# Windowed attention of a two-block fp32 model: stacked query halves, doubled keys, values with both halves side by side

## The reference, cut to what matters

```
q, k, v = jnp.split(h @ w_qkv, [Hq * d, Hq * d + Hkv * d], axis=-1)   # Hq 16, Hkv 4, d 64
q = apply_rope(q...); k = apply_rope(k...)
s = jnp.einsum('bnqhgd,bnchd->bnhgqc', q, kb) * (d ** -0.5)           # kb: 3 blocks of 128 keys
s = jnp.where(|kpos - qpos| <= 128 and 0 <= kpos < S, s, -jnp.inf)
m = jnp.maximum(jnp.max(s, axis=-1), sink)
e = jnp.exp(s - m)
pr = e / (jnp.sum(e, axis=-1) + jnp.exp(sink - m))
o = jnp.einsum('bnhgqc,bnchd->bnqhgd', pr, vb)
return o @ w_o
```

## Time and profile before

| | |
|---|---|
| median of three runs | 2090.47 us (2089.05 to 2092.75) |
| the profiled execution: its span | 2087.8 us; its time is not given apart, the median lies 2.7 us over the span |
| PE busy | 2043.2 us, 98% of the span |
| DVE, ACT, POOL busy | 1224.2, 941.6, 904.8 us |
| the second attention, from k0 to the last product with the values | about 722 to 888 us from the start |

### The profile page before, as it was taken

How to read it: one execution, slowest core, us unless ns; L and a number is a source line. 1 busy time by engine, 2 the same in 40 slices (tenths; PEclk the granted TensorE clock), 3 DMA queues, 4 the chain that set the end, 5 groups by cost and what they waited for, 6 DMA issues and landing times.

```text
span 2087.8 us, 28730 instructions
## 1 busy us (share of the span) xinstructions
PE 2043.2 (98%) x9976; PEld 1684.1 (81%) x9976; DVE 1224.2 (59%) x1842; ACT 941.6 (45%) x1495; POOL 904.8 (43%) x660
## 2 busy tenths in 40 slices
PE   7999999999999999899999999999999999999999
PEld 6777788888887878788888887878888788888887
DVE  6677857546265789856636266548879473213222
ACT  5456645434245567635424245535742544322222
POOL 4322235545456431044645456444215454455454
PEclk9999999999999999999999999999999999999999
DMA  4222122332323211022333223222103222232323
GB/s 169 81 76 76 48 75 98 103 101 91 101 91 121 81 61 32 31 91 81 101 101 101 92 99 112 91 81 92 39 23 107 85 91 92 90 110 92 101 91 111
DMA packets 52756, 183.21 MB, mean 88 GB/s; under 512 B 6576, under 2 KB 6832, under 8 KB 52656
## 3 DMA queue, kind: packets, MB, share of 16 engines
q1 hardware_dynamic: 51072, 177.76, 25.9%
q10 hardware_dynamic: 1584, 4.07, 0.5%
HBM read 176.04 MB, written 2.10 MB: 85 GB/s over the span
## 4 chain that ended last, share of the span: by engine, by line
PE 53%; issue 24%; POOL 13%; DVE 7%; ACT 2%; POOLq 0%; DVEq 0%; DMA 0%; ACTq 0%; SPq 0%
PE PS L544 52%; POOL wlo L536 13%; DVE AR L1915 1%; PE PS L773 1%; DVE AR L1918 0%; DVE acc L1630 0%; DVE ptlo L1805 0%; DVE AR L1797 0%; DVE nmax L1753 0%; ACT AR L1187 0%; DVE AR L2277 0%; ACT AR L1323 0%; DVE AR L1931 0%; DVE Blo L1935 0%; DVE Blo L2281 0%
## 5 line engine op out<-in xcount | busy, mean ns | idle before, releaser
L536 POOL TENSOR_TENSOR wlo<-raw,whi 128x512 fp32r<-128x512 f32 x656 | 904.6, 1402 | 1169.7 <-ACT whi L1090 1168.5
L544 PE MATMUL PS<-Bhi,whi 128*128 128x512 f32 x2352 | 927.7, 394 | 17.2 <-DVE Blo L1623 10.8
L544 PE MATMUL PS<-Blo,whi 128*128 128x512 f32 x2352 | 917.6, 390 | 0.0
L544 PE MATMUL PS<-Bhi,wlo 128*128 128x512 f32 x2352 | 917.4, 390 | 0.0
L1090 ACT ACTIVATE whi<-raw 128x1024 fp32r<-128x1024 f32 x328 | 345.2, 1056 | 510.7 <-PE PS L544 435.4
L544 PEld LDWEIGHTS PS<-Bhi,whi 128*128 128x128 f32 x2352 | 442.5, 188 | 123.1 <-issue 14.1
L544 PEld LDWEIGHTS PS<-Bhi,wlo 128*128 128x128 f32 x2352 | 442.6, 188 | 93.7
L544 PEld LDWEIGHTS PS<-Blo,whi 128*128 128x128 f32 x2352 | 443.0, 188 | 89.3 <-issue 0.5
L1614 DVE TENSOR_TENSOR AR<-PS,R 128x512 f32<-128x512 f32 x170 | 115.3, 690 | 235.9 <-PE PS L544 224.1
L1670 DVE TENSOR_TENSOR X<-X,PS 128x512 f32<-128x512 f32 x88 | 60.3, 687 | 227.2 <-PE PS L544 226.5
L1915 DVE SCALAR_TENSOR_TENSOR AR<-AR,par_sb 128x511 f32<-128x511 f32 x88 | 117.6, 1336 | 8.8 <-ACT AR L1323 8.8
(11 more groups left out here) (237 smaller groups left out, 2069.1 us busy)
## 6 DMA issues: line engine op xcount, KB each, us to landing
raw<-in_weights SPq DMA_DIRECT2D x328, 512.0 KB, 3.2
AR<-AR SPq DMA_DIRECT2D x56, 64.0 KB, 2.0
X<-in_xT ACTq DMA_DIRECT2D x4, 512.0 KB, 6.9
out<-X SPq DMA_DIRECT2D x8, 256.0 KB, 3.0
AR<-in_pT ACTq DMA_DIRECT2D x2, 512.0 KB, 3.9
par_sb<-in_parameters ACTq DMA_DIRECT2D x1, 314.0 KB, 8.5
AR<-in_positions ACTq DMA_DIRECT2D x1, 256.0 KB, 8.3
con_sb<-in_constants ACTq DMA_DIRECT2D x1, 198.5 KB, 8.1
```

The source lines that it names most:

```text
L536: ins = pool.tensor_tensor(wlo[:, j, c], raw[:, j % RAWS, c], f32(whi[:, j, c]), ALU.subtract)
L544: return pe.matmul(out, w, x, start=start, stop=stop)
```

## The change

The two parts of a query head now stand one above the other: `stackq[:, b, s, :]` holds 64 rows of one part and 64 rows of the other of head s. `stackk` holds the high part of a key head twice, on both halves of the rows, and the low part twice. So two matmuls over 128 rows give all four products of a head, where three over 64 rows gave three. The mask of a head is one matmul over 128 rows. `stackq` and `stackk` are filled by transfers from `qk`, which SP issues: four of 64 x 2 x 512 for a key tile (`stack_keys`), four of 64 x 512 for a query tile (`stack_queries`), each kind after a certain `load`. The PE waits for them (`qstacked`, `kstacked`) before the first scores of a pair.

The 64 zero columns of a head's values now hold the low part of the values (the padding is not cleared any more). `outputs` is then two matmuls for each block of keys and head, 12 in place of 18, and each head has its own half of bank 7 for two steps. ACT moves one 64-row half of each into place (`evacuate_part`, two instructions of 64 x 256 after every second step), DVE adds the other (`add_parts`, two instructions of 64 x 256). PE waits for that before it writes bank 7 again.

```diff
@@ -200 @@
-        qkhi = sb("qkhi", [P, 2, 2, T], F32R)
-        qklo = sb("qklo", [P, 2, 2, T], F32R)
+        qk = sb("qk", [P, 2, 2, 2, T], F32R)
+        qkhi, qklo = qk[:, 0], qk[:, 1]
@@ -290 @@
+        stackq = Bhi[1][:, TB * T:].rearrange("p (b s t) -> p b s t", b=2, s=2)
+        stackk = Blo[1][:, :].rearrange("p (h l t) -> p h l t", h=4, l=2)
@@ -515 @@
+            def stack_keys(kb):
+                n = QT0[2] + 2 * kb
+                sp.wait_ge(q_ready, n + 1)
+                for s in range(2):
+                    rows = slice(64 * s, 64 * s + 64)
+                    for to in range(0, P, 64):
+                        sp.dma_start(f32(stackk[to:to + 64, 2 * kb + s, :, :]), f32(qk[rows, :, kb, 1, :]))\
+                            .then_inc(kstacked[kb], 16)
+            def stack_queries(j):
+                b = j % 2
+                sp.wait_ge(q_ready, QT0[2] + (1 if j == 0 else j + 2) + 1)
+                if j >= 2:
+                    sp.wait_ge(score_done, SC0[2] + 8 * (j - 1))
+                for s in range(2):
+                    rows = slice(64 * s, 64 * s + 64)
+                    for half in range(2):
+                        to = 64 * (half ^ s)
+                        sp.dma_start(f32(stackq[to:to + 64, b, s, :]), f32(qk[rows, half, b, 0, :]))\
+                            .then_inc(qstacked[b], 16)
+            begin, of_k, of_q = SLAB0["kq2a"] // 4 * 4, SLAB0["kq2a"], SLAB0["kq2"]
+            end = -(-(of_q + NPROJ[2] + 6) // 4) * 4
+            stacks = {of_k + 6: (stack_keys, 0), of_k + 7: (stack_queries, 0),
+                      of_q + 6: (stack_keys, 1)}
+            for j in range(1, 8):
+                stacks[of_q + j + 6] = (stack_queries, j)
...
+            for s in range(begin, end):
+                load(s, s % RAWS, s - 1)
+                if s in stacks:
+                    stack, n = stacks[s]
+                    stack(n)
@@ -710 @@ (scores)
+                if qb == 0 and kind == 2:
+                    pe.wait_ge(qstacked[b], 64 * (j // 2 + 1))
+                    if j % 4 == 0:
+                        pe.wait_ge(kstacked[kb], 64)
...
+                    if kind == 2:
+                        for half in range(2):
+                            mm(out, stackq[:, b, s, cols], stackk[:, 2 * kb + s, half, keys],
+                               half == 0, False)
...
+                        mm(blocks[:, at[0]:at[-1] + 1:2, :], constR[:, 0, :], constR[:, c:c + len(masks), :],
+                           False, True).then_inc(score_done, 1)
+                        continue
@@ -780 @@ (outputs)
+                if kind == 2:
+                    pe.wait_ge(o_ready, OP0[2] + g // GROUP)
...
+                    for s in range(2):
+                        head = 2 * (j // 4) + s
+                        for n, (_, k, a, b) in enumerate(spans):
+                            r, c = row_of(kind, g, s, k), (a - q0) * P
+                            out = PS[:, 7, 2 * P * s + c:2 * P * s + (b - q0) * P]
+                            for half, buf in enumerate((pthi, ptlo)):
+                                last = mm(out, vhi[:, k, head, :], keys_of(buf, kind, g)[:, r, c:c + (b - a) * P],
+                                          n == 0 and half == 0, n == len(spans) - 1 and half == 1)
@@ -1234 @@ (scalar)
+            def evacuate_part(e):
+                act.wait_ge(pv_done, PV0[2] + e + 1)
+                j, c = e // 2, slice(2 * P * (e % 2), 2 * P * (e % 2) + 2 * P)
+                act.activation(OA[0:64, j, c], PS[64:128, 7, 0:2 * P], ACT.Copy)
+                act.activation(OA[64:128, j, c], PS[0:64, 7, 2 * P:4 * P], ACT.Copy).then_inc(part_ready, 1)
@@ -1838 @@ (vector)
+            def add_parts(e):
...
+                    ins = tt(OA[rows, j, c], OA[rows, j, c], PS[rows, 7, 2 * P * s:2 * P * s + 2 * P], ALU.add)
@@ -1892 @@ (vector, attention)
+                        if g and g % GROUP == 0:
+                            add_parts(g // GROUP - 1)
@@ -2076 @@
-            zero_padding("v2")
```

More of the change, by code:

```diff
@@ L340, in build @@
         hinv_ready, hspread = sem("hinv_ready"), sem("hspread")
+        qstacked = [sem(f"qstacked{n}") for n in range(2)]
+        kstacked = [sem(f"kstacked{n}") for n in range(2)]
+        part_ready = sem("part_ready")
         dve_tap = [sem(f"dve_tap{c}") for c in range(CT)]
@@ L363, in build, with padded @@
         PAIRS = {1: 8, 2: 8, 3: 4}
-        def padded(stage, B, src, t):
+        def padded(stage, B, src, t, low=False):
             nh = 4 if stage == "v2" else 8
@@ L372, in padded @@
             s = src.rearrange("p (n two c) -> p n two c", two=2, c=64)
-            return [(v[:, :, u, 64 * u:64 * u + 64], s[:, :, u, :]) for u in range(2)]
+            at = [64 * u if not low else 64 - 64 * u for u in range(2)]
+            return [(v[:, :, u, at[u]:at[u] + 64], s[:, :, u, :]) for u in range(2)]
         def band(kind, qb):
@@ L517, in _ @@
                 load(s, s % RAWS, s - 1)
-            with sp.Fori((first + NPROJ[1] + 3) // 4, SLABS // 4) as i:
+            def stack_keys(kb):
[23 more added lines that the diff above has]
+                stacks[of_q + j + 6] = (stack_queries, j)
+            with sp.Fori((first + NPROJ[1] + 3) // 4, begin // 4) as i:
+                for j in range(4):
+                    load(4 * i + j, j % RAWS, 4 * i + j - 1)
+            for s in range(begin, end):
[3 more added lines that the diff above has]
+                    stack(n)
+            with sp.Fori(end // 4, SLABS // 4) as i:
                 for j in range(4):
@@ L712, in scores @@
                 first, nb, masks = band(kind, qb)
-                if g == 0 and kind > 1:
+                if g == 0 and kind == 3:
                     pe.wait_ge(swapped_ready, 2)
@@ L737, in scores @@
                     out = PS[:, score_bank(kind, n), 0:nb * P]
+                    if kind == 2:
+                        for half in range(2):
+                            mm(out, stackq[:, b, s, cols], stackk[:, 2 * kb + s, half, keys],
+                               half == 0, False)
+                        blocks = out.rearrange("p (b c) -> p b c", c=P)
+                        at, c = [block for block, _ in masks], masks[0][1]
+                        mm(blocks[:, at[0]:at[-1] + 1:2, :], constR[:, 0, :], constR[:, c:c + len(masks), :],
+                           False, True).then_inc(score_done, 1)
+                        continue
                     last = mm3(out, qkhi[rows, b, 0, cols], qklo[rows, b, 0, cols],
@@ L796, in outputs @@
                 spans.sort(reverse=True)
+                if kind == 2:
+                    for s in range(2):
[6 more added lines that the diff above has]
+                                          n == 0 and half == 0, n == len(spans) - 1 and half == 1)
+                    last.then_inc(pv_done, 1)
+                    return
                 work = [(k, a, b, 0) for _, k, a, b in spans]
@@ L1163, in values @@
                         act.wait_ge(rcol_ready, 1 + NORMS.index({"v1": "attn0", "v2": "attn1", "v3": "mix"}[stage]))
[L1164 to L1166 removed]
+                        if stage == "v3":
+                            act.wait_ge(pad_ready, 4)
                     for t in VALUES[stage, hf]:
@@ L1277, in attention @@
                             output_high(OA, c)
-                    if g % 4 == 0 and g:
+                    if kind == 2 and g % GROUP == 0 and g:
+                        evacuate_part(g // GROUP - 1)
+                    if kind != 2 and g % 4 == 0 and g:
                         evacuate(kind, g // 4 - 1)
@@ L1687, in values_low @@
                         else:
-                            lo = padded(stage, Blo, PS[:, bank, 0:width], t)
+                            lo = padded(stage, Bhi if stage == "v2" else Blo, PS[:, bank, 0:width], t, stage == "v2")
                             hi = padded(stage, Bhi, PS[:, bank, 0:width], t)
@@ L1839, in add_half @@
                 tt(X[:, m, :], X[:, m, :], PS[:, bank, :], ALU.add).then_inc(tile_free[bank], 1)
+            def add_parts(e):
+                j, c = e // 2, slice(2 * P * (e % 2), 2 * P * (e % 2) + 2 * P)
+                dve.wait_ge(part_ready, e + 1)
+                for s in range(2):
+                    rows = slice(64 * s, 64 * s + 64)
+                    ins = tt(OA[rows, j, c], OA[rows, j, c], PS[rows, 7, 2 * P * s:2 * P * s + 2 * P], ALU.add)
+                    if s == 0:
+                        own.step(ins)
+                ins.then_inc(o_ready, 1)
             def output_low(src, c):
@@ L1894, in attention @@
                     if kind == 2:
+                        if g and g % GROUP == 0:
+                            add_parts(g // GROUP - 1)
                         for c in OSPLIT.get(g, ()):
                             output_low(OA, c)
+                if kind == 2:
+                    add_parts(steps // GROUP - 1)
             def feed_forward(l):
```

22 lines of the change are left out of this document (11 added, 11 removed).

## The result

The changed kernel takes 2180.9 us (median of 4 runs, 2179.4 to 2182.3), the kernel before 2089.8 (4 runs): **1.0438 times as long, 95% interval 1.0423 to 1.0453**, some 91 us more.

A forecast was written before the change was run, and what follows sets the result against it. PE and DVE were taken to run in step, neither with room. Seven pairs at 10.5 us (73.5), plus 7 at the start, minus 0.4, make 80; with the span of 2087.8 and 2.7 that is 2171 us, range 2130 to 2197.

The forecast's parts named there:

- The forecast case: Second attention: PE waits for query transfers queued behind a weight load, 10.5 us per pair for seven pairs; 2171 us, chance 0.72.
- The wait: PE at each later query tile waits for four transfers behind the load in SP's queue: 8.6 us, bounds 3.9 to 10.8.
- the weight step comes earlier: Rival: a faster PE lets the load go out sooner, wait about 5 us, no slow clock; 2128 us, chance 0.13.
- landing: Time from a query transfer's issue to its arrival, taken as 2.0 us from the first attention's transfers.
- From the wait's end to the next maxima: After PE resumes, DVE begins the following step's maxima 5.6 us later, 8.0 us later than before, without the clock.
- PE's saving: Fewer matmuls save PE 11.5 us in the values and 8 us in the scores, about 19.5 us if PE is the bound.
- DVE's adds: Four add instructions of 64 x 256 per pair on DVE, 0.33 us each: 1.3 us per pair, at most 1.7.
- The clock: After each stop PE runs a stretch at half clock, making its work longer by 1.7 to 3.4 us; 2.3 taken.
- The start: First scores of the second attention: PE begins 6.1 us late plus 1 us for the clock, +7 us.
- Hidden transfers: Rival: transfers are in place before PE asks, only DVE's adds cost, 8 pairs x 1.3 us; 2100 us, chance 0.04.
- Faster: Rival: PE is the bound, adds fall into DVE's gaps and transfers are in time; 2071 us, chance 0.03.
- Longer issue: Rival: a transfer of 64 rows takes twice as long to issue, 2.4 us more per pair; 2195 us, chance 0.08.

The follow-up runs named there:

- the first experiment: The changed kernel with the four transfers of each later query tile and of the second key tile ahead of the load in SP's queue: 2153.0 us, ratio 1.0318.
- the values alone: The kernel before with only the new values (12 matmuls, ACT's copies, DVE's adds), scores as before, no transfers: 2095.6 us, ratio 1.0048.
- the kernel with the keys moved: Changed kernel, later transfers ahead of the load, projection a step earlier, second key tile's transfers issued after pair 2's queries: 2126.3 us, ratio 1.0174.

## Why the prediction came out as it did

**The forecast case held.** The wait for the transfers in SP's queue behind the load is the mechanism: PE waits at each of the eight tiles, the profile shows all of it in the places named, and the kernel with the transfers ahead of the load gains back 28 us. What lies ahead of the second attention did not move: of the first 722 us PE is busy for 700.0 in the kernel before and 701.0 in the changed one. Behind it 1194 us of the two, taken 92 us apart, have PE busy for 1183.6 and 1184.2.

**The sum.** By the rows of `q_low` the changed kernel is 803.4 - 780.2 = 23.2 us late at pair 2's tile, and 943.9 - 863.0 = 80.9 at pair 7's. The spans differ by 2179.9 - 2087.8 = 92.1. So the start and pair 1 cost 23.2, five pairs 57.7 (11.5 each), the rest 11.2. The prediction had 7 + 10.5 - 0.4 = 17.1, then 52.5, then 10.5. Half of what was missing lies at the start, half in the pairs.

**The wait: 8.6 forecast, 10.3 measured** (pair 2; 10.2 to 10.9 in pairs 2 to 7). Its steps, measured from T: the load at 3.2 (forecast 4.27), the first transfer at 3.6 (4.6), the last issue at 5.4 (6.5), PE's resuming at 9.1 (8.6). The load did come a little earlier, as the rival "the weight step comes earlier" had it, by 1.1 us and not by the 3.6 that its wait of 5 would take. The term that was mis-sized is the **landing**: 3.7 in place of the 2.0 taken from the earlier trace rows. The two errors, the load 1.1 too late and the landing 1.7 too short, go against each other, so that the end of the wait is only 0.5 us off is in part luck. (The upper bound of 10.8 is 10.7 by its own terms.) The transfers in rows 8 had no load just ahead of them; the first experiment gives 2.3 for these transfers in that position. The Trainium skill, "DMA: Bandwidth & Descriptors", section "Anatomy of one DMA", fits 2.0 us plus the bytes at 436 GB/s (for transfers issued by GpSimd), which for 128 KB is an estimate of 2.3. The trace gives the same number where nothing is ahead, though SyncE issues these transfers, and is 1.4 above it behind a load. Another 1.2 us of the longer wait are no loss of their own: PE came to it 1.2 us before T, where before it came together with T. PE's saved matmuls fit that: they let PE come earlier to a wait that ends at the same time.

**From the wait's end to the next maxima.** DVE's maxima were forecast 8.0 us late plus 2.3 for the clock. In pair 2 they are at T + 16.99 and not T + 6.19, 10.8 late for 10.3; the 0.5 is the later end of the wait. The whole period is 11.2 us longer for this pair and 11.5 on average, so 0.4 to 0.7 comes in the steps behind, where 0.2 was forecast.

**PE's saving.** A step of three blocks takes 847.89 - 846.90 = 0.99 us for its scores (1.17 before, forecast 0.96). There is no gap at its exit and one of 0.05 at most at its entry; with that, counted as the 1.17 was, it is 1.04:

```profile
846.90 0.56 PE L593 MATMUL PS<-Blo,Bhi 128*128 128x384 f32 x2
847.30 0.28 PE L593 MATMUL PS<-constR 128*128 128x256 f32 x1
847.42 0.51 PE L593 MATMUL PS<-Blo,Bhi 128*128 128x384 f32 x2
847.77 0.28 PE L593 MATMUL PS<-constR 128*128 128x256 f32 x1
847.89 0.39 PE L593 MATMUL PS<-Bhi,whi 128*128 128x512 f32 x1
```

So the stacked form does win time on PE, somewhat less than forecast: 0.13 to 0.18 in a step of three blocks against 0.2. The prediction had weighed here a rule against a row. With the switches unpriced, one more pass for the two heads would have made this step 0.18 us longer (0.15 on average), and it became shorter. That is the side of the gaps in rows 6, and of the drain on a change of mode that the Trainium skill, "TensorEngine Tiling (Array Packing)", Key Properties, gives. How much of it could reach the end of the kernel is not shown: no run has the stacked scores without new stops of PE. For the values, where a run exists, 3.4 of 11.5 us were left when DVE's adds were taken away.

**DVE's adds: 1.3 forecast, 1.28 measured** per pair. That agrees by luck. The adds last 0.41 each and start 0.44 apart, the upper end of 0.42 and not the 0.33 taken, so 1.66 per pair; the run without them still has two operations of 0.14, and 1.66 - 0.28 = 1.38 is near the 1.28.

**The clock: 2.3 forecast, 2.0 measured** between PE's resuming and the next step's scores. Taking the low clock away gave 1.7 there, because it fell again in one pair of five, and 1.2 per pair in the period. The prediction's reading of its row is worded the wrong way round: a mean of 0.66 over 5 us is 1.6 us at full and 3.4 at half clock, and it was the 3.4 that it used. The profile of the stretch after a stop (813 to 820 us, then 820 to 826, in the changed kernel) has the half clock in its first part alone:

```profile
813.00:820.00 7.00, 6.77 (x35) 6.13 (x36) 3.06 (x10) 1.47 (x4) 0.00 (x0) 0.71 0.00 0
820.00:826.00 6.00, 5.11 (x35) 4.36 (x33) 5.39 (x17) 5.20 (x15) 0.00 (x0) 1.00 0.02 5
```

**The start: 7 forecast.** SP's queue there, key tile 0, the load, query tile 0, the next load, and then PE:

```profile
736.46 3.40 SPq L536 DMA_DIRECT2D Blo<-qk  x4
739.90 1.06 SPq L508 DMA_DIRECT2D raw<-in_weights  x1
741.01 3.14 SPq L550 DMA_DIRECT2D Bhi<-qk  x4
744.19 0.58 SPq L508 DMA_DIRECT2D raw<-in_weights  x1
```

```profile
748.90 0.80 PE L593 MATMUL PS<-Blo,Bhi 128*128 128x256 f32 x2 [10.63 <-DMA Bhi<-qk]
```

PE goes on at 748.90, 8.2 us later than before, where 6.1 were forecast. An issue took 0.85 us on average (3.40 / 4) for the keys and 0.79 for the queries, not 0.63, and the load's issue 1.06, not 0.33. SP issued slower here, where more was in flight, than in the steps; that the one is the cause of the other no run shows. PE's start was forecast for 746.8.

**Pair 1** was priced like the others and is the other half of the start's excess: 785.03 is 12.4 us after its `q_low` (772.67), not 9.1. SP's queue has four key transfers and a slow load (0.59 us to issue) ahead of it. Of the 3.3 us more, 0.7 is a later first issue, 0.8 a slower issue of the four (3.18 us for 2.38), and the rest a slower landing. How much of it is the keys' stays open: where the projection was earlier, moving them away made the landing 1.2 us faster and the kernel no faster.

**The rivals.** Weight step earlier (2128): its sign was seen, its size not. Hidden transfers (2100): the values alone gave 2095.6, near its price for the adds, but no arrangement hid the transfers without a new stop, and the best of them took 2126. Faster (2071): refuted by the result, and its premise by the values alone: 11.5 us less work for PE and 1.3 us more per pair for DVE made the kernel slower. Longer issue (2195): not in the steps (2.38 us for four, 2.41 in rows 8), though at the start.

## What to carry to other kernels

Before removing work from an engine that is 98% busy, look whether another one runs in step with it: here DVE was 91% busy in the same stage, and 96 matmuls fewer gave 3.4 us of 11.5 at best, while 1.3 us of adds per pair came out in full. A transfer put between two steps that followed each other within 0.05 us cost its place in the queue, its issue and its landing, all of it. Hiding it took a step of lead for the chain behind it, and each way tried here to give it that lead took the cover or the bank of something else. In SP's queue the order of issue mattered twice, for when a transfer is issued and for how fast it lands.

## What the runs showed of the hardware

- A transfer of 128 KB from SBUF to SBUF lands 2.3 us after its issue with nothing ahead of it (2.2 to 2.4), and 3.7 to 3.8 us in pair 2 when issued 0.4 us behind a load of 512 KB in the same queue (all eight tiles: median 3.9, 3.6 to 5.4, the longest with key transfers ahead as well).
- Useless work can make a kernel faster. 36 matmuls in a wait of 5.3 us kept the granted clock at 1.00 instead of 0.86 and took 15.7 us off. Filling the longer wait of 10.3 us, with the clock at 0.99 instead of 0.80, gave 6.2 us.
- A longer stop cost less clock. After stops of 5.3 us PE's work up to the next scores took 2.8 us more than at full clock; after stops of 10.3 us 1.4 to 2.9, 2.0 on average, because more of the stretch at half clock (0.50 from about 806.9 to 817.1 us) lay in the stop.
- Stops of 2.4 and 1.6 us per pair were enough for a mean clock of 0.84 over 80 us, which is lower than with one stop of 5.3 us per pair (0.86). Stops of 2.6 and 0.8 us per pair (the kernel with the keys moved) left it at 0.94 over the same stretch. So short stops can lower the mean clock as much as a long one, and two of them close together did more than a longer and a very short one.
